# Three stages of a decoder step as one program, weight casts on GpSimd, and fill tiles loaded from ScalarE's queue

## What is computed

```python
h = xn @ w_in        # fq fk fv ff fz  hq hf hi hz  mq mz  ga gb gm
scores = q @ k.T * Dh**-0.5 + c[i] - c[j]        # c = cumsum(log f), causal
S = exp(bl) * S + (k * exp(bl - b)).T @ v        # recurrence, by chunks
mixed = sigmoid(ga) * ya + sigmoid(gb) * yb + sigmoid(gm) * ym
y = rmsnorm(x + mixed @ w_o)
```

## Time and profile before

| | |
|---|---|
| median of 3 runs | 3039.75 us (3035.96 to 3053.45) |
| the profiled execution | 3042.43 us |
| its span, first to last instruction | 3040.4 us |
| PE busy | 2802.5 us, 92% |
| weight loads, DVE, ACT, POOL | 76%, 52%, 36%, 24% |
| mean granted clock of PE | 0.967 of full speed |

### The profile page before, as it was taken

The page is one execution under the profiler, slowest core; times in us unless marked ns, Lnnn a source line. Parts: engine busy times, 40 slices in busy tenths (PEclk is TensorE's granted clock), DMA queues, the critical chain, the costliest instruction groups (busy, mean ns, idle before and its releaser), DMA issues. The chain is left out here.

```text
span 3040.4 us, 38617 instructions
## 1 busy us (share of the span) xinstructions
PE 2802.5 (92%) x13880; PEld 2295.6 (76%) x13880; DVE 1577.6 (52%) x3007; ACT 1098.7 (36%) x2086; POOL 728.0 (24%) x743
## 2 busy tenths in 40 slices
PE   7889988899998889898789998999999978999998
PEld 5668767677776778687678877888888866888887
DVE  5414578433341467665345555656664546444544
ACT  1212111333332345443245554555554223232322
POOL 6027655123223343433020061011020014000000
PEclk9999989899998999999999999999999989999999
DMA  5576678756653656565745564555444546333331
GB/s 167 222 237 202 210 222 262 239 155 186 194 166 129 217 198 232 188 213 183 234 140 163 160 187 140 163 158 154 142 140 130 198 174 194 124 110 115 116 109 49
DMA packets 290765, 526.33 MB, mean 173 GB/s; under 512 B 110270, under 2 KB 135423, under 8 KB 269327
## 3 DMA queue, kind: packets, MB, share of 16 engines
q1 hardware_dynamic: 237519, 403.41, 42.2%
q0 software_dynamic: 17440, 55.98, 6.5%
q10 hardware_dynamic: 35616, 64.47, 5.6%
HBM read 411.09 MB, written 112.68 MB: 172 GB/s over the span
## 5 line engine op out<-in xcount | busy, mean ns | idle before, releaser
L2528 PE MATMUL fill_out<-keep_hi,fill_x 128*128 128x512 f32 x2112 | 739.8, 413 | 87.4 <-DMA fill_x<-x_tiles 47.2
L2528 PEld LDWEIGHTS fill_out<-keep_hi,fill_x 128*128 128x128 f32 x2112 | 391.7, 193 | 160.8 <-issue 36.1
L2528 PE MATMUL fill_out<-keep_lo,fill_x 128*128 128x512 f32 x1056 | 433.8, 411 | 3.9 <-PEq L3215 3.9
L413 ACT ACTIVATE fox_pt_hi<-fox_turned 128x512 fp32r<-128x512 f32 (+1 forms) x320 | 170.1, 531 | 321.2 <-PE fox_turned L363 319.3
L466 DVE TENSOR_TENSOR fox_pt_lo<-fox_turned,fox_pt_hi 128x512 fp32r<-128x512 f32 (+1 forms) x320 | 194.9, 609 | 169.2 <-ACT fox_pt_hi L413 166.7
L452 DVE CUSTOM_DVE_ANT_0 fox_probs<-fox_scores,fox_bias 128x512 f32<-128x512 f32 (+2 forms) x320 | 187.6, 609 | 106.1 <-PE fox_scores L352 56.2
L2528 PEld LDWEIGHTS fill_out<-keep_lo,fill_x 128*128 128x128 f32 x1056 | 203.6, 193 | 35.7 <-issue 4.3
L2150 ACT ACTIVATE in_stage<-in_out 128x512 f32<-128x512 f32 (+1 forms) x119 | 70.4, 594 | 433.8 <-PE in_out L99 385.2
L2628 POOL CAST keep_hi<-fill_raw 128x512 fp32r<-128x512 f32 x48 | 30.2, 628 | 652.3 <-PE fill_out L2539 616.9
L363 PE MATMUL fox_turned<-ident,fox_probs 128*128 128x128 f32 x1088 | 173.2, 274 | 7.1 <-ACT fox_probs L404 6.4
L97 PE MATMUL mf_out<-mf_w_hi,mf_t_hi 128*128 128x512 f32 x408 | 166.7, 409 | 9.0 <-DVE mf_w_lo L3031 8.1
(11 more groups left out here) (382 smaller groups left out, 6391.2 us busy)
## 6 DMA issues: line engine op xcount, KB each, us to landing
fill_x<-x_tiles SPq DMA_DIRECT2D x132, 1024.0 KB, 5.4
dc_slot<-in_cache_fox_k_dram SPq DMA_DIRECT2D x128, 256.0 KB, 3.9
dc_slot<-in_cache_fox_v_dram SPq DMA_DIRECT2D x128, 256.0 KB, 3.3
in_raw<-in_w_in_dram POOLq DMA_DIRECT2D x104, 256.0 KB, 3.6
plain<-fill_stage ACTq DMA_DIRECT2D x96, 256.0 KB, 5.5
mf_gate<-plain SPq DMA_DIRECT2D x96, 256.0 KB
turned<-in_stage ACTq DMA_DIRECT2D x64, 256.0 KB, 3.9
fill_raw<-in_w_in_dram POOLq DMA_DIRECT2D x56, 256.0 KB, 3.2
```

The source lines that it names most:

```text
L413: act.activation(pt_hi[:, zeta % PT_SLOTS, skip:BANK], bank_of(st)[:, skip:BANK], ACT.Copy).then_inc(hi_ready, 1)
L2528: ins = pe.matmul(self.out[n % self.OUTS][:], x, w, start=(k == 0 and term == 0), stop=(ends and term == 2))
```

## The change

- `recur_prompt`, `attend_prompt` and `attend_memory` are emitted into one block with one cleanup. In place of the ends of the programs stand waits on semaphores: `recur.computed` (all chunks done) before the first queries' load, the first key transposes and the constants of the attention on POOL; `recur.all_stored` before the first scores and exponentials; `prompt.scores_done`, `banks_free` and `all_stored` for the memory stage, whose keys, values and queries are now loaded at the last head's last key step of the attention. These explicit waits are there because tiles of the stages share memory.
- The recurrence has no tail slots. The attention's opening has ten fill slots with 24, 24, 12 x 4 and 16 x 4 matmuls (240 on both sides of the boundary before, 160 now), and the loop 1552 in place of 1472. SP loads queries and keys first, values and bias behind the first piece's store, z behind the second's.
- All casts are on POOL: 24 in the recurrence and 104 in `project_and_decode`. There `split_at` puts slice k into tick k in both passes.
- The fill's x tiles from the third on are loaded from ACT's queue, `load_behind` ahead of the eviction, not from SP's.
- In the memory stage z and o_rows have changed places, and the second z is loaded once the attention has stored all.

```diff
@@ attend_prompt
-    steps = [("fill", 0)] + [("queries", 0, b) for b in range(QUADS)] + [("values", 0, b) for b in range(QUADS)]
+    steps = [("open", 0), ("fill", 0), ("open", 1), ("fill", 1), ("open", 2)] + [("queries", 0, b) for b in range(QUADS)]
     for b in range(QUADS):
-        steps += [("fill", 1 + b), ("keys", 0, b)]
+        steps += [("keys", 0, b), ("fill", 2 + b)]
+    steps += [("values", 0, b) for b in range(QUADS)]
     for i in range(4):
-        steps += [("score", 0, i, 0), ("fill", 1 + QUADS + i), ("exp", 0, i)]
+        steps += [("score", 0, i, 0), ("fill", 2 + QUADS + i), ("exp", 0, i)]
...
+                    if st == ("open", 0):
+                        recur.computed(sp)
+                        fill.wait_stored(sp, needed)
+                        load_queries(sp, 0)
+                        for n in range(2):
+                            load_keys(sp, *quads[n])
+                    if st == ("open", 1):
+                        recur.store_state(sp)
+                        recur.store_rows(sp, 0)
+                        load_values(sp, 0)
+                        load_bias(sp, 0)
+                    if st == ("open", 2):
+                        recur.store_rows(sp, 1)
+                        for n in range(2):
+                            load_z(sp, *quads[n])
@@ recur_prompt
         late(len(chunks) - 1)
         for piece in range(PIECES):
             post(BLOCKS - 1, piece)
-            tail(piece)
...
-        fill.begin(fill.spread(matmuls, 2 * (len(chunks) + AHEAD)) + fill.spread(last_matmuls, TAIL), True)
+        fill.begin(fill.spread(matmuls, 2 * (len(chunks) + AHEAD)))
...
+        def computed(eng):
+            eng.wait_ge(state_ready, len(chunks))
+            eng.wait_ge(o_taken, len(chunks))
@@ attend_memory
+            prompt.scores_done(sp)
             fill.wait_stored(sp, needed)
             sp.dma_start(k_rows[:], mem_k.rearrange("(t p) c -> p t c", p=P)).then_inc(kv_loaded, 16)
             sp.dma_start(v[:], mem_v.rearrange("(t p) c -> p t c", p=P)).then_inc(kv_loaded, 16)
-            for blk in range(2):
-                load(blk)
+            load_q(sp, 0)
+            load_z(sp, 0)
+            load_q(sp, 1)
             paged.sync_start(sp)
+            prompt.sync_rest(sp)
@@ project_and_decode
-            return (n - 1) * U + (k // 2 if n < G else k)
+            return (n - 1) * U + k
...
-                def low(m):
+                def split_slice(m):
                     hi, lo = w_ring.at(ring_at[m])
+                    pool.wait_ge(raw_loaded[m % RAWS], 16 * ((m - KT) // RAWS + 1))
+                    ring_free(pool, m)
+                    pool.tensor_copy(hi, raw[m % RAWS][:]).then_inc(cast, 1)
                     pool.wait_ge(cast, m - KT + 1)
                     pool.tensor_tensor(lo, raw[m % RAWS][:], hi.bitcast(F32), ALU.subtract).then_inc(split, 1)
...
-                def high(m):
-                    act.wait_ge(raw_loaded[m % RAWS], 16 * ((m - KT) // RAWS + 1))
-                    ring_free(act, m)
-                    act.activation(w_ring.at(ring_at[m])[0], raw[m % RAWS][:], ACT.Copy).then_inc(cast, 1)
@@ Filler
     def scalar(self, act, slot):
         for n in self.units_ending(self.until(slot), self.until(slot + 1)):
+            self.load_behind(act, n)
             self.evict(act, n)
...
-    def sync(self, sp, slot):
-        for n in self.units_ending(self.until(slot), self.until(slot + 1)):
...
-                self.load_x(sp, m + self.RING)
+    def load_behind(self, queue, n):
+        g = self.group_of(self.first_unit, n)
+        m = self.first_x[g] + n - self.first_unit[g]
+        if not self.is_sample(n) and m + self.RING < self.first_x[-1]:
+            self.load_x(queue, m + self.RING)
@@ the counts and the call
-MATMULS = {"recur": 1340, "recur_last": 96, "fox_first": 144, "fox": 1472, "fox_last": [10, 12], "memory_first": 16}
+MATMULS = {"recur": 1340, "fox_first": [24, 24] + [12] * 4 + [16] * 4, "fox": 1552, "fox_last": [10, 12], "memory_first": 16}
...
-                with nc.cleanup_on_exit():
-                    recur_prompt(nc, core, turned[PT["hq"]], turned[PT["hf"]], plain[PN["hi"]][0:T, :],
+                with nc.cleanup_on_exit(), nc.Block() as block:
+                    recur = recur_prompt(nc, core, block, turned[PT["hq"]], turned[PT["hf"]], plain[PN["hi"]][0:T, :],
```

More of the change, by code:

```diff
@@ L99, in product, with attend_prompt @@
     return pe.matmul(out, a[0], b[1], start=False, stop=last)
[L102 removed]
+def attend_prompt(nc, core, block, queries, fox_k, fox_v, z_fox, neg_c, gated, fill, matmuls, first_matmuls, last_matmuls, recur, needed):
     QUADS = NT // 4
@@ L488, in recur_prompt, with rows, load_queries @@
-def recur_prompt(nc, core, queries, gates, values, z_hg, gain, gated, state_out, fill, matmuls, last_matmuls, needed):
+        def rows(dram, head, first, count):
+            return dram[first * P:(first + count) * P, head * FD:(head + 1) * FD].rearrange("(t p) c -> p t c", p=P)
+        def load_queries(sp, head):
+            if head >= 1:
+                sp.wait_ge(q_ready, head * QUADS)
+            for half in range(2):
+                sp.dma_start(q_raw[half * FD:(half + 1) * FD, :],
+                             rows_of(queries, head * FD, FD)).then_inc(q_loaded, 16)
@@ new lines, in load_values, with load_keys @@
+        def load_values(sp, head):
+            if head >= 1:
+                sp.wait_ge(v_ready, head * QUADS)
+            sp.dma_start(v_raw[:], rows(fox_v, head, 0, NT)).then_inc(v_loaded, 16)
+        def load_keys(sp, head, b):
+            n = head * QUADS + b
+            if n >= 2:
+                last = quads[n - 2]
+                sp.wait_ge(turned_ready, turn_at["keys", last[0], last[1]] + 1)
+            for half in range(2):
+                sp.dma_start(k_raw[n % 2][:, :, half * FD:(half + 1) * FD], rows(fox_k, head, 4 * b, 4)
+                             ).then_inc(k_loaded[n % 2], 16)
@@ L490, in recur_prompt @@
+        return AttentionEnd(lambda sp: sync_steps(sp, steps[split_at:]), scores_done, banks_free, all_stored)
+def recur_prompt(nc, core, block, queries, gates, values, z_hg, gain, gated, state_out, fill, matmuls):
     CH = 4
@@ L895, in attend_memory, with load_z, store @@
-def attend_memory(nc, core, queries, mem_k, mem_v, z_mem, gated, last, fill, matmuls, first_matmuls, needed):
+        def load_z(sp, n):
+            if n >= 2:
+                sp.wait_ge(rows_ready, n - 1)
+            sp.dma_start(z[n % 2][:], z_hg[n * 2 * P:(n + 1) * 2 * P, :].rearrange("(c p) n -> p c n", p=P)
+                         ).then_inc(z_loaded[n % 2], 16)
+        def store(sp, blk, piece):
+            n = blk * PIECES + piece
+            sp.wait_ge(rows_ready, n + 1)
+            sp.dma_start(gated[n * 2 * P:(n + 1) * 2 * P, :].rearrange("(c p) n -> p c n", p=P),
+                         o_rows[blk % 2][:, 2 * piece:2 * piece + 2, :]).then_inc(stored[blk % 2], 16)
+            if n + 2 < BLOCKS * PIECES:
+                load_z(sp, n + 2)
@@ L897, in attend_memory @@
+        return RecurrenceEnd(computed, store_state, lambda sp, piece: store(sp, BLOCKS - 1, piece), all_stored)
+def attend_memory(nc, core, block, queries, mem_k, mem_v, z_mem, gated, last, fill, first_matmuls, needed, prompt):
     ST = NM // P
@@ L921, in attend_memory @@
         paged = PagedEnd(nc, core, ctx, *last)
-        fill.begin([first_matmuls] + fill.spread(matmuls - first_matmuls, NT + 1))
         def sem(name):
@@ new lines, in _, with value, extra @@
+        @block.sync
+        def _(sp):
+            def value(u):
+                blk = u // BLK
+                if u % BLK == BLK - 1:
+                    sp.wait_ge(rows_ready, u + 1)
+                    sp.dma_start(rows(gated, blk), o_rows[blk % 2][:]).then_inc(stored[blk % 2], 16)
+                    if blk + 2 < BLOCKS:
+                        load_q(sp, blk + 2)
+                        load_z(sp, blk + 2)
+            prompt.all_stored(sp)
+            load_z(sp, 1)
+            def extra(u):
+                paged.sync(sp, u)
+            walk(nothing, nothing, value, extra)
+            paged.sync_end(sp)
+            fill.wait_stored(sp, len(fill.groups))
+            for i in range(2):
+                sp.wait_ge(stored[i], 16 * (BLOCKS // 2))
```

1316 lines of the change are left out of this document (625 added, 691 removed).

## The result

The changed kernel takes 3024.6 us (median of nine runs, 3010.1 to 3031.4) against 3045.5 for the kernel before in nine runs beside it: a ratio of 0.9933, with a 95% interval of 0.9917 to 0.9949. That is 20 us, 0.67% less. A second profile of the same kernel has a span of 3021.4.

A forecast was written before the change was run, and what follows sets the result against it. PE, busy 92% of the span, was taken as the bound, with its idle stretches and half-clock restarts. Terms A to I and +2 for the end cleanup sum to −25.4, taking the median 3039.75 to 3014 us; range 2984 to 3046.

The forecast's parts named there:

- D: Start of the recurrence: third x tile on ACT's queue avoids SP's queued loads, −5 us (−9 to 0).
- F: Recurrence's three group changes: PE waits for POOL's low slices instead of ACT's eviction, +1 us (−6 to +8).
- G: Recurrence to attention: start, x and slow-clock losses shrink, but x(7) comes late, −13 us (−28 to −5).
- I: Attention to memory stage: program start, query and x waits mostly go, −9 us (−12 to −3).
- A: Start of projection stage: gather issued some 5 us earlier, PE's scan wait shrinks, −6 us (−8 to −1).
- B: Rest of the projection's first pass: POOL's waits for ACT's casts vanish, casts load POOL, −6 us (−8 to +20).
- C: Projection's second pass: bunched last slices cost POOL 0.63 us more each, +1 us (0 to +6).
- E: Recurrence: x loads wait behind ACT's own work in three places, +8.6 us (0 to +12).
- H: Attention loop: every unit adds 0.33 us to ACT's queue, +1 us (−2 to +6).
- (1): Rival: ACT's queue is no obstacle to x loads, so E is 0 and G −28; 2991 us, chance 0.2.
- (3): Rival: merged program gives its gain back to late x loads on ACT; 3038 us, no difference, chance 0.2.
- (2): Rival: POOL bounds the decode once about nine tenths busy between 240 and 480; 3058 us, slower, chance 0.14.

The follow-up runs named there:

- the mixture: Changed kernel with the recurrence's casts on ACT and x loaded by SP from the attention loop on: 3009.5 us, ratio 0.9885; again 3002.8 us, 0.9874.
- POOL doubled: Changed kernel with the low part of each projection-stage slice computed twice on POOL: 3103.3 us, ratio 1.0202 to the kernel before.

## Why the prediction was right, and where it was not

Forecast were 25 us less, measured 20 (0.67%, where 0.8% were forecast). Direction and range were right, and so were the mechanisms of D, F, G and I. That the sum came so near is luck in part: the first pass gave 8 us more than A and B say, C cost 9 more, E 9 less, F 10 more, G gave 3 less, H cost 3 more, and 5 at the end of the projection stage were not in the sum. Of the signs named ahead most came out (no wait on the scan, x waits of 31.6 in sum, POOL's fill lows at 35.0, no gap over 2 us at the memory stage), but none of them could tell C, E and F from their measured sizes.

- **A to C, projection stage, −11: −10, by two errors that cancel.** The mean of nine traces with the new stage is 803.2 us, that of two with the old one 813.3: −10.1, and the timed run with this part alone gave −10 (with the shorter end below in it). A and B, −12 together, measured −20, beyond the −16 of their bounds together (first pass 405.4 us against a mean of 425.7). **C, +1: mis-sized, it measured +10** (second pass 397.9 against 387.7), outside its range of 0 to +6. Its mechanism was named, low slices in bunches at the group ends, but priced as if PE's matmuls covered nearly all of it; PE waits 9.0 us there. A is seen at once: the matmul behind the scan runs with no wait in the changed kernel (in the two traces of the mixture 3.7 and 3.4 us are left of it).

```profile
185.97 0.28 PE L1729 MATMUL in_small<-dc_slot,dc_later 128*128 128x8 f32 x2
```

  The gather is issued at 174.46, 5.4 us earlier than in the earlier trace rows (7.2 counted from the stage's start), where "some 5" was forecast. Four slices stand ahead of it in the trace before, not the six of the prediction, and two after. The page table's load held it 4.37 us until 174.46, which I had named as the case of −1. The gain came all the same, since that load moved up too: SP issued it at 171.19, at 176.24 before, in a run of loads that starts 0.1 us behind POOL's last mask (167.15 behind 167.07, and 172.13 behind 172.05 before). What the prediction lacked is that the two parts gain only together, and that the casts are paid for in the second pass.
- **The end of the stage** was not in the sum: −4.6.
- **D, −5.** The two stages around x(2): 45.5 to 37.8, −7.6, near the −9 end. ACT issued the tile at 969.18, and PE's second stall was 2.47 us against 9.24 in the earlier trace rows. Two runs with x back on SP's queue had 45.0 and 44.6. By the Trainium skill, DMA: Bandwidth & Descriptors, section Queues, rings and completion order, the queue rows are served in turn, from which the prediction had half of the bandwidth for the tile and −9. The trace agrees in direction: its 1 MB landed within 7.9 us of the issue (14.3 before), about 133 GB/s while the DMA engines moved 400, nearer a third than half.

```profile
969.18 0.33 ACTq L2591 DMA_DIRECT2D fill_x<-x_tiles  x1
...
977.06 0.70 PE L2541 MATMUL fill_out<-keep_hi,fill_x 128*128 128x512 f32 x2 [2.47 <-DMA fill_x<-x_tiles]
```

- **E, +8.6: mis-sized, it measured about 0.** With casts on ACT the recurrence takes 427.4 us with x on SP and 427.3, 431.2, 426.6 and 427.5 with x on ACT; with casts on POOL 439.2 and 437.8 against 437.8 and 440.4. The stalls exist where I put them, but are 1.4 us at most, 3.4 in all (1.8 and 4.2 in the second trace). The failed step is the row that I took for the price: the start of the eviction behind an x load in the earlier trace rows is not when ACT would issue the load. ACT's timeline just behind the second of the three places:

```profile
1138.06 0.33 ACTq L2591 DMA_DIRECT2D fill_x<-x_tiles  x1
1138.24 0.42 ACT L752 ACTIVATE hg_level<-hg_level 128x256 f32<-128x256 f32 x1
...
1139.77 0.59 ACT L2568 ACTIVATE fill_stage<-fill_out 128x512 f32<-128x512 f32 x1
```

  The exponentials from 1138.24 on come before the load in the program's order, yet the load is issued first. In these rows waits hold a load back (the root's for DVE: the load before this one was issued at 1134.54, just behind the root at 1134.39), not the work queued on the engine: a table load and two exponentials stand between that root and the eviction, and the prediction charged them to the load.
- **F, +1: mis-sized, it measured +11.** With the casts back on ACT the kernel is 12 us faster, and the recurrence 7 to 13 us shorter. The mechanism was as told (the late end moves to POOL): POOL's waits rose by 21 us and ACT's fell by 18. The step that failed is the −4 for fewer long stalls and slow restarts. The stalls got more in number, 13 over 1 us in the recurrence against 7 before and 8 or 9 with the casts on ACT, and against the latter PE was idle 4 to 9 us more and busy, at the lower clock, 1 to 3 us more. The range for it ended at +8.
- **G, −13: −9.6.** The opening's mean is 61.8 us in seven traces with x on ACT, against 89.7 in four of the old one, 18.3 of it moved. The step that ACT issues x(7) only behind the last root is right to the row:

```profile
1447.60 0.21 ACT L777 ACTIVATE hg_root<-hg_stat 128x8 f32<-128x8 f32 x1 [6.64 <-DVE hg_stat L847]
1447.60 0.33 ACTq L2591 DMA_DIRECT2D fill_x<-x_tiles  x1
...
1454.20 1.19 PE L2541 MATMUL fill_out<-keep_hi,fill_x 128*128 128x512 f32 x2 [10.15 <-DMA fill_x<-x_tiles]
```

  "Some 10 us" were forecast. A second stall of 2.7 to 4 us behind the keys was not. And taking the cause away did not bring the −28 of the bound, as the run with x on SP showed.
- **H, +1: +4.4** (826.4 us in six traces against 803.7 in four, less 18.3). 6 us of the loop are ACT's issue, at the bound of +6; the +1 rested only on no wait for ACT being among PE's long ones before.
- **I, −9: −10**, and the end **+2: +1.6** (from the last turned gates to the end of the span 44.8 us, 43.2 before). SP issued the memory keys at 2301.21, 35 us before PE wanted them, and one wait of 1.38 is left.

```profile
2301.21 0.55 SPq L980 DMA_DIRECT2D mem_k_rows<-out_dram  x1
...
2336.22 1.99 PE L1038 MATMUL mem_scores<-mem_keys,mem_q 128*128 128x256 f32 x8 [1.38 <-DVE mem_keys L1071]
```

The measured terms add up to −10.1 − 4.6 − 7.6 + 0 + 11 − 9.6 + 4.4 − 10 + 1.6 = −25, at the edge of the interval of the timed −20 (−15 to −25). Against the prediction's −25.4 these terms agree only in their sum.

Of the rivals, (1) fell: E is 0 as it says, but G is not 28. (3) was wrong in its mechanism: x on ACT is worth nothing in total (0.9933 with all x on SP, 0.9933 with it on ACT), for D's 7.6 and H's 6 cancel. What gave gain back was the casts, some 10 us in the second pass of the projection and 11 in the recurrence. (2) did not occur in the first pass, where it was placed. Its condition, nine tenths busy, is not what decides: the casts cost PE 10 us in the second pass with POOL 38% busy there. The contention that the Trainium skill names (GPSIMD Engine Reference, section 8, Key points) did not grow with POOL's load: the 18 multiplications of the earlier trace rows took 2.43 us in the mean before, 2.41 and 2.37 in the two traces of the changed kernel and 2.13 with POOL doubled. One of DVE's updates of the sample's state, two SBUF operands, took 1.57 us in the mean of eight before, then 0.68, 1.07 and 1.35. Single stretched operations are still there (4.6 us for the multiplication of the earlier trace rows at 274.87 and 352.15 in the changed kernel), where the 6.17 was the longest before.

## What to carry to other kernels

Where a serial loop on one engine (wait, cast, subtract, issue the next load) gates the bound engine's next group, price the loop by its length times its turns plus the restarts of the clock, not as a wait that merely changes its name. A low busy share of that engine over a stage is no licence: here the casts cost PE 10 us in a pass where POOL was 38% busy, because its slices come due together at the group changes. Cut a stage where its work changes kind before summing it; a gain of 20 and a loss of 10 looked like one gain of 10. A load that ACT issued was held back by the waits ahead of it in program order and not by the engine's queued work, and the work behind it started 0.43 us after it. Merging programs pays through what can be loaded before the boundary (18 us here), and each part that came with it should be timed by itself: here one cost 12 us, and two gained nothing without each other.

## What the runs showed of the hardware that I had not expected

- A DMA issue on ACT's queue overtook activations that precede it in the program: issued at 1138.06, with five of them starting from 1138.24 to 1139.47.
- The program boundary behind the projection stage: SP's first issue of the next program came 5.7 us behind the start of PE's last matmul when POOL had been idle for long, and 11.6 us behind POOL's last instruction, in four kernels, when POOL worked late. Over all traces PE's pause there is 10.5 to 10.9 us in the one kind and 15.2 in the other.
- The same code's projection stage varied from 794.4 to 811.1 us over nine executions, while the attention loop repeated within 1.4 us over six. The variation is in the first pass (396.9 to 414.2 us); the second repeated within 4 us. The page cache's loads are issued in both (157 of 289 in the first), so they alone don't explain it.
